# The down weights of the experts go to GpSimd's DMA queue, gate and up stay on SyncE's

## What is computed

```python
def moe_swiglu(h, w_router, wg, wu, wd):
    logits = (h @ w_router).astype(jnp.float32)
    top_v, top_i = lax.top_k(logits, TOP_K)
    ...
    act = jax.nn.silu(jnp.einsum('bnd,edf->bnef', h, wg)) * jnp.einsum('bnd,edf->bnef', h, wu)
    act = act * gates.astype(h.dtype)[..., None]
    return jnp.einsum('bnef,efd->bnd', act, wd)
```

## Time and profile before

| | us |
|---|---|
| median of 3 runs | 1752.54 |
| lowest, highest | 1752.37, 1757.84 |
| the profiled execution, its own time | 1752.99 |
| its span in the profile | 1751.2 |
| expert stage, from the first expert product to the last | about 876 to 1715 |

### The profile page before, as it was taken

The page is one execution under the profiler, slowest core; times in us unless marked ns, Lnnn a source line. Parts: engine busy times, 40 slices in busy tenths (PEclk is TensorE's granted clock), DMA queues, the critical chain, the costliest instruction groups (busy, mean ns, idle before and its releaser), DMA issues.

```text
span 1751.2 us, 24750 instructions
## 1 busy us (share of the span) xinstructions
PE 1560.6 (89%) x9147; PEld 1030.0 (59%) x9148; DVE 767.1 (44%) x1243; ACT 583.8 (33%) x994; POOL 75.9 (4%) x92
## 2 busy tenths in 40 slices
PE   4798989999999898989687999899998999999771
PEld 1684577888887585567522566545654677676220
DVE  0574676333333573766700455334453443333015
ACT  1433445233331542441200544334443333333001
POOL 2010011000000010020000000000000000000002
PEclk8899999999999899999898999999999999999885
DMA  9245536343243445465389999999999477777992
GB/s 340 97 144 169 193 110 216 119 144 117 100 144 122 144 143 188 169 207 195 108 313 389 355 388 362 388 350 360 317 371 369 173 265 262 254 270 261 395 370 80
DMA packets 202174, 414.09 MB, mean 236 GB/s; under 512 B 11336, under 2 KB 52296, under 8 KB 202032
## 3 DMA queue, kind: packets, MB, share of 16 engines
q1 hardware_dynamic: 195712, 390.64, 62.0%
q0 software_dynamic: 5264, 18.04, 3.2%
q10 hardware_dynamic: 1056, 3.54, 0.5%
HBM read 400.64 MB, written 11.53 MB: 235 GB/s over the span
## 4 chain that ended last, share of the span: by engine, by line
PE 75%; DMA 8%; DVE 6%; issue 4%; ACT 3%; SPq 2%; ACTq 1%; POOL 0%; DVEq 0%; POOLq 0%
PE ps L1966 27%; PE ps L2368 5%; PE ps L2285 5%; PE ps L2362 4%; PE ps L2286 4%; PE ps L2289 4%; DMA qkv<-in_w_moe_up 3%; PE ps L2408 3%; PE ps L2414 3%; PE ps L1898 2%; PE ps L2310 2%; DMA gu_ring<-in_w_moe_up 2%; PE ps L2313 2%; PE ps L2316 2%; SPq L679 2%
## 5 line engine op out<-in xcount | busy, mean ns | idle before, releaser
L1966 PE MATMUL ps<-d_ring_parts,scratch_parts 128*128 128x512 f32 (+1 forms) x444 | 172.4, 388 | 14.3 <-DVE hT_parts L1241 9.5
L1800 DVE TENSOR_TENSOR cst<-cst,ps 128x256 f32<-128x256 f32 (+2 forms) x89 | 32.9, 369 | 270.8 <-ACT cst L1098 270.8
L1966 PE MATMUL ps<-gu_ring_parts,scratch_parts 128*128 128x512 f32 (+1 forms) x336 | 128.0, 381 | 0.0
L1966 PE MATMUL ps<-d_ring_parts,hT_parts 128*128 128x512 f32 (+1 forms) x312 | 118.4, 380 | 0.0
L1966 PE MATMUL ps<-gu_ring_parts,o_parts 128*128 128x512 f32 x264 | 103.8, 393 | 0.0
L1966 PEld LDWEIGHTS ps<-d_ring_parts,scratch_parts 128*128 128x128 f32 x444 | 84.6, 190 | 32.5 <-issue 9.3
L2362 PE MATMUL ps<-gu_ring,hT 128*64 128x512 f32 x288 | 74.8, 665 | 30.1 <-issue 18.5
L1106 ACT ACTIVATE cst<-ps 128x128 f32<-128x128 f32 (+1 forms) x51 | 16.1, 316 | 235.4 <-PE ps L2384 221.3
L1757 DVE TENSOR_TENSOR gu_ring_parts<-gu_ring,qkv_parts 128x1024 fp32r<-128x1024 f32 x54 | 64.3, 1223 | 64.8 <-PE ps L2368 23.4
L1098 ACT ACTIVATE cst<-ps 128x256 f32<-128x256 f32 (+2 forms) x89 | 30.7, 345 | 166.3 <-PE ps L2289 74.8
L2285 PE MATMUL ps<-qkv_parts,o_parts 128*128 128x512 f32 x182 | 75.5, 415 | 4.0 <-DVE gu_ring_parts L1757 4.0
(11 more groups left out here) (414 smaller groups left out, 3369.5 us busy)
## 6 DMA issues: line engine op xcount, KB each, us to landing
gu_ring<-in_w_ada SPq DMA_DIRECT2D x48, 1024.0 KB, 7.4
gu_ring<-in_w_moe_gate SPq DMA_DIRECT2D x96, 512.0 KB, 7.9
gu_ring<-in_w_moe_up SPq DMA_DIRECT2D x96, 512.0 KB, 9.4
gu_ring<-in_w_moe_down SPq DMA_DIRECT2D x96, 512.0 KB, 9.2
d_ring<-in_w_moe_gate SPq DMA_DIRECT2D x48, 512.0 KB, 9.4
d_ring<-in_w_moe_up SPq DMA_DIRECT2D x48, 512.0 KB, 10.4
d_ring<-in_w_moe_down SPq DMA_DIRECT2D x48, 512.0 KB, 7.1
gu_ring<-in_w_in SPq DMA_DIRECT2D x16, 1024.0 KB, 7.4
```

Of the source, the lines that this page charges most:

```text
L1966: ins = pe.matmul(out, a, w, start=(start and n == 0), stop=(stop and n == 2))
```

## The change

SyncE loads gate/up granules alone, in the old order and with the old waits. GpSimd loads the down granules: 4 and 5 of the first expert after `out_mm` reaches 12, granule 10 after its load of norm parameters, and the rest in a loop of its own with registers of its own for the experts' numbers. `freed` is unchanged but for the engine that waits. Each of the 33 positions has its own landing semaphore in place of one for each of the 11 slots. The early gathers keep their place in GpSimd's stream, behind what is loaded there now. Which slot a position has, and which products run in which order, stays.

```diff
-        ring_landed = [sem(f"ring_landed{k}") for k in range(RING)]
+        ring_landed = [sem(f"granule_landed{k}") for k in range(GRANULES)]
...
+        def freed(eng, t, pos):
...
+            kind, _, _, k = granule_of(pos)
+            if kind == "gu":
+                eng.wait_ge(gu_freed, t * GU_GRANULES + (k + 1))
+            elif pos == GRANULES - 1:
+                eng.wait_ge(y_mm, t * HELD + HELD)
+            else:
+                eng.wait_ge(d_freed, t * D_GRANULES + (k + 1))
...
             sp.wait_ge(out_mm, 12)
-            for pos in range(RING):
-                if pos == 9:
-                    sp.wait_ge(gather_mm, 16)
-                load_granule((0, 0), pos)
+            for pos in GATE_UPS:
+                if pos < RING:
+                    if pos == 9:
+                        sp.wait_ge(gather_mm, 16)
+                    load_gate_up((0, 0), pos)
...
+                now = experts_of(sp, t)
+                for pos in GATE_UPS:
+                    if pos >= RING:
+                        freed(sp, t, pos - RING)
+                        load_gate_up(now, pos)
...
-                else:
-                    pool.wait_ge(gather_mm, 16)
                 if l == 0:
                     rstds(3, 1)
                 else:
+                    pool.wait_ge(out_mm, 12)
+                    for pos in (4, 5):
+                        for f in range(2):
+                            pool.dma_start(ring[pos][:, D * f:D * f + D],
+                                           w_moe_down[0, 0][FC * (pos - 4) + P * f:FC * (pos - 4) + P * f + P, :]
+                                           ).then_inc(ring_landed[pos], 16)
+                    pool.wait_ge(gather_mm, 16)
                     load_ln(1, 1)
+            DOWNS = [pos for pos in range(GRANULES) if granule_of(pos)[0] == "d"]
+
+            def load_down(experts, pos):
+
+                _, sc, q, _ = granule_of(pos)
+                e = experts[sc % 2 if sc < NSUPER - 1 else 0]
+                for f in range(2):
+                    r0 = FS * sc + FC * q + P * f
+                    pool.dma_start(ring[pos % RING][:, D * f:D * f + D], w_moe_down[0, e][r0:r0 + P, :]).then_inc(
+                        ring_landed[pos], 16)
+
+            load_down((0, 0), 10)
+            pool.wait_ge(sched_ready, 1)
+            with nc.Fori(0, NE - 1, engines=[pool.engine], hint_back_edge=True) as t:
+                now = experts_of(pool, t)
+                for pos in DOWNS:
+                    if pos >= RING:
+                        freed(pool, t, pos - RING)
+                        load_down(now, pos)
+                then = experts_of(pool, t + 1)
+                for pos in DOWNS:
+                    if pos < RING:
+                        freed(pool, t, pos + GRANULES - RING)
+                        load_down(then, pos)
...
             pool.wait_ge(rows_placed, 1)
             pool.wait_ge(rows_out, STORES * NE)
...
-                        act.wait_ge(ring_landed[pos % RING], t * (32 * (GRANULES // RING)) + 32 * (pos // RING + 1))
+                        act.wait_ge(ring_landed[pos % GRANULES], t * 32 + 32 * (pos // GRANULES + 1))
```

More of the change, by code:

```diff
@@ L669, in _, with load_gate_up @@
                             d_landed[ch % D_SLOTS], 16)
-            def load_granule(experts, pos):
-                kind, sc, q, _ = granule_of(pos)
+            def load_gate_up(experts, pos):
+                _, sc, q, _ = granule_of(pos)
                 e = experts[sc % 2 if sc < NSUPER - 1 else 0]
[L675 to L681, removed]
-                else:
-                    for f in range(2):
-                        r0 = FS * sc + FC * q + P * f
-                        sp.dma_start(dst[:, D * f:D * f + D], w_moe_down[0, e][r0:r0 + P, :]).then_inc(landed, 16)
@@ L687, in freed @@
[L687 to L699, removed]
@@ L701, in _ @@
-            sp.wait_ge(out_mm, 12)
-            for pos in range(RING):
-                if pos == 9:
-                    sp.wait_ge(gather_mm, 16)
-                load_granule((0, 0), pos)
+                dst, landed = ring[pos % RING], ring_landed[pos]
+                nk, w = (2, FS) if sc < NSUPER - 1 else (4, FC)
+                for a, src in enumerate((w_moe_gate[0, e], w_moe_up[0, e])):
+                    sp.dma_start(dst.rearrange("p (k a f) -> p k a f", k=nk, a=2)[:, :, a, :],
+                                 src.rearrange("(k p) f -> p k f", p=P)[:, nk * q:nk * q + nk, FS * sc:FS * sc + w]
+                                 ).then_inc(landed, 16)
@@ L706, in _ @@
+            GATE_UPS = [pos for pos in range(GRANULES) if granule_of(pos)[0] == "gu"]
+            sp.wait_ge(out_mm, 12)
+            for pos in GATE_UPS:
[3 more added lines that the diff above has]
+                    load_gate_up((0, 0), pos)
             sp.wait_ge(sched_ready, 1)
             with nc.Fori(0, NE - 1, engines=[sp.engine], hint_back_edge=True) as t:
[L708 to L719, removed]
+                now = experts_of(sp, t)
[3 more added lines that the diff above has]
+                        load_gate_up(now, pos)
@@ L720, in _ @@
+                then = experts_of(sp, t + 1)
+                for pos in GATE_UPS:
+                    if pos < RING:
+                        freed(sp, t, pos + GRANULES - RING)
+                        load_gate_up(then, pos)
+            now = experts_of(sp, NE - 1)
+            for pos in GATE_UPS:
+                if pos >= RING:
+                    freed(sp, NE - 1, pos - RING)
+                    load_gate_up(now, pos)
             for i in range(NT):
@@ L800, in _ @@
                 else:
-                    load_ln(1, 1)
+                    pool.wait_ge(out_mm, 12)
[5 more added lines that the diff above has]
+                    pool.wait_ge(gather_mm, 16)
+                    load_ln(1, 1)
+            DOWNS = [pos for pos in range(GRANULES) if granule_of(pos)[0] == "d"]
+            def load_down(experts, pos):
+                _, sc, q, _ = granule_of(pos)
+                e = experts[sc % 2 if sc < NSUPER - 1 else 0]
[8 more added lines that the diff above has]
+                for pos in DOWNS:
+                    if pos >= RING:
+                        freed(pool, t, pos - RING)
+                        load_down(now, pos)
+                then = experts_of(pool, t + 1)
+                for pos in DOWNS:
+                    if pos < RING:
+                        freed(pool, t, pos + GRANULES - RING)
+                        load_down(then, pos)
+            now = experts_of(pool, NE - 1)
+            for pos in DOWNS:
+                if pos >= RING:
+                    freed(pool, NE - 1, pos - RING)
+                    load_down(now, pos)
             pool.wait_ge(rows_placed, 1)
```

7 lines of the change are left out of this document (5 added, 2 removed).

## The result

| | before | after |
|---|---|---|
| median | 1755.19 us (4 runs) | 1787.57 us (4 runs, 1779.41 to 1797.07) |
| ratio | | 1.0172, 95% interval 1.0130 to 1.0214 |
| profiled execution, its span | 1752.99, 1751.2 us | 1786.47, 1784.7 us |
| second set of runs (11 and 6) | 1759.47 us | 1784.09 us, ratio 1.0148 (1.0121 to 1.0175) |

The change makes the kernel 1.5 to 1.7% slower. I had forecast 1757 us in a range of 1744 to 1770; the result lies outside. In the changed kernel L679 has become L693 and L685 L817; L2362, L2368, L2384, L2408, L2414 and L2477 each stand 36 lines further down (L2398, L2404, L2420, L2444, L2450, L2513), as do L807, L1727 and L1822 (L843, L1763, L1858).

The account below looks back on a forecast made before the run. TensorE was taken as the busiest engine (89%), with narrow experts bound by DMA bytes. Terms 0 + 0 + 0 + 0 + 4.5 us on the profiled 1752.99 us gave 1757.5, or 1757 us beside the median; range 1744 to 1770 us.

Parts of the forecast that it names:

- Issue: Expert stage: 176 down DMAs move to GpSimd at 0.58 us each, no stall; SyncE's saved issues were hidden: 0.
- semaphores: Landing of granules: 33 semaphores in place of 11, with the same number of waits: 0.
- VectorE beside: Each expert's three VectorE copies could lock out GpSimd's DMAs, by the skill's rule at most 1.7 us an expert.
- How the two queues share: Expert stage: downs issued after a gate/up can overtake it; taken as 0, ends -7 and +16 us.
- In byte-bound experts it is 0 for the same reason: Narrow experts: overtaking costs 0, since the load backlog outlasts TensorE's work to free the next slots.
- My backlog of 8 us: At an overtaken fourth gate/up granule: three granules queued, longer than the 5.7 us TensorE needs to free the next slots.
- Wide experts: loads land long before use.: Wide experts, where TensorE is always busy: overtaking by downs costs 0.
- Gathers: Last expert: early gathers behind GpSimd's last downs delay VectorE's folds and the result's copy: +4.5 us, ends 0 and +12.
- Rival 1: Expert stage: downs rob gate/ups of bandwidth; new waits at 975 to 1145 us exceed twice 6.7 us; 1773 us, chance 0.12.
- The general signs of a wrong forecast: Gate/up waits below 20 or above 45 us, any down wait, slow GpSimd DMAs, narrow experts above 400 or below 380 GB/s.
- Rival 4: Two TensorE idle times, if code loading, grow 4 us each through a third party at the engines: 1765 us, chance 0.06.
- rival 2: Expert stage: faster, with fewer gate/up waits and holes, 401 GB/s and folds at the low end: 1740 us, chance 0.17.

Follow-up runs that it names:

- sems: The kernel before with one landing semaphore for each of the 33 granules, all loads still on SyncE's queue: 1757.20 us, ratio 0.9999.
- hold_next: The changed kernel with only the next expert's downs (granules 4, 5, 10) held until its gate/up granule 3 or 9 has landed: 1774.08 us, 1.0074.
- in_turn: The changed kernel, but GpSimd issues a down only after SyncE has issued every gate/up ahead of it: 1772.40 us, ratio 1.0072.
- the repeat: The changed kernel run once more, unaltered, beside a later group of runs: 1784.09 us, ratio 1.0148.
- half_rows: The changed kernel, each down DMA carrying one half of the columns of 256 rows, runs of 2 KB instead of 4: 1800.95 us, 1.0247.
- swap: The changed kernel with queues exchanged: GpSimd loads gate/ups, SyncE downs, early gather 0 ahead of granule 30: 1810.46 us, ratio 1.0290.
- both: The kernel before, each granule's first DMA by SyncE, second by GpSimd, old order, gathers 0 and 1 ahead of granule 28: 1776.11 us, 1.0127.

## Why the prediction was wrong

- **Issue, semaphores, VectorE beside: right.** 0.59 us a down DMA against the forecast 0.58, and no pause like the 10.31 us of the earlier trace rows. sems is at 0.9999. The lock that the Trainium skill (SBUF — State Buffer, "DVE blocks DMA") warns of would hold up GpSimd's DMAs. All 172 down DMAs at L817 took 0.53 to 0.54 us each, so no trace of it shows here.
- **How the two queues share: the step that failed.** I had written 0, with ends of -7 and +16 us. The case in it was right: a gate/up overtaken by downs, 5.4 us late. Granule 21 is that case, 16.4 - 11.0 = 5.4 us. That it meets the forecast's 5.4 us so exactly is luck, since the shares were not equal. Four things in it were wrong. (1) "In byte-bound experts it is 0 for the same reason": the first expert, byte-bound, lost 11.4 us, more than any other place but one. (2) I let only the two downs of the same super overtake. But a queue that does not wait for gate/ups runs on to the next expert, and beside granule 31 there were five downs. hold_next and in_turn put this at about half of the whole loss. (3) I argued that a late TensorE costs nothing since the engines work on bytes that must be moved anyway. They do until the ring is full; then the share falls to 0.58 over 30 us where it was 0.91. A ring bounds how far ahead a queue can work, so work done early on the wrong half is lost when the right half is late. My backlog of 8 us was compared with TensorE's next few steps and not with the time until the ring is full. (4) I assumed shares of one half each. The queues took turns by packets, so in bytes it was 2.0 to 1 for GpSimd's, and 3.7 to 1 beside granules 30 and 31, where the three longest waits lie. I had the lengths of the rows and did not use them.
- **"Wide experts: loads land long before use."** No wait for weights there before; after, 8.9 us in eight waits from 1362 to 1657 us, and the third group is 13.0 us longer, the largest item: 8.9 us of these waits, 4.2 us more busy time, 2.1 us more idle time with no releaser shown at the start of the last expert, less 2.2 us of a wait for VectorE that is gone. I had no term for it.
- **The clock: missed.** No term of the sum turned longer waits into slower matmuls; busy time rose by 13.1 us (6.5 in the repeat), part of it in the clock's dip behind the longest wait.
- **Gathers: the delay right, the path not.** The first gather went behind the last downs, and VectorE's fold waited for it, as forecast. But the 4.5 us of the sum were the copy of the result, delayed by VectorE's third fold; this copy (1749.94 us) waited 2.83 us for TensorE and not for a fold. The 4.50 us that appeared are a wait of TensorE's last turn, for which I had 1.6 us (1709.75 to 1711.3), and 3.65 us of them are VectorE's idle time with no releaser shown. That both are 4.5 is luck. The last expert as a whole is 2.2 us longer.
- **Rival 1** (gate/up robbed, 1773 us) was the true case in its mechanism, to which I gave 0.12, but not in its place, and its bound of 16 us was too small. Its own test failed: TensorE's gate/up waits from 975 to 1145 us are 3.4 us, not above twice 6.7; the loss is at the ends of experts and in the third group. The general signs of a wrong forecast, waits for gate/ups above 45 us and any wait for a down, came true: 47.9 and 4.9.
- **Rival 4** (code loading, two longer idle times) did not come true: the idle times before the first products of the first and the last expert are 9.97 and 10.52 us, 20.5 in total, against 18.5 before and 20.1 in sems, which has one queue.
- **Rule on issuing engines.** I used the rule of the Trainium skill (DMA: Bandwidth & Descriptors, Issuing engines are not separate DMA queues) that more issuing engines only save issue time against rival 2. That they gain no rate holds here (394 to 396 GB/s after, 393 before, in narrow experts). It does not say that they cost nothing; what the page says on taking queues in turn, which I had not weighed, bears on that.

Still open: the rest of in_turn's 0.7% (the two queues should still share by packets in it, but no run takes that away alone), what GpSimd's queue costs as such, and why half_rows and swap are so slow. No kernel of the study beat the one before.

## What to carry to other kernels

A stream of loads in order of use on one queue is a schedule, and a second queue removes it: whatever is not waited for runs ahead as far as the ring lets it, and in a byte-bound stage that is taken from the one load that the compute engine stands on. If two queues are wanted, tie their issue order together with a count (here that gave half of the loss back); if one is enough, keep it. If they are loaded at the same time, work out their shares from the sizes of their packets in a trace: the queue with the smaller packets gets the smaller share. When costing an overtaking, ask how far the free queue can run, not only what stands next to the late load, and add the slower clock behind each long wait.

## What the runs showed of the hardware

- Where two queues had work, they moved equal numbers of packets: 351 and 352, 426 and 427 in the changed kernel, 271 and 273 in swap. In bytes that was 2.0 to 1, 3.7 to 1 and 1 to 1, by the sizes of the packets. In both, equal loads in the same order landed with medians of 9.1 us (GpSimd's) and 12.5 us (SyncE's).
- GpSimd's packets stayed at 3.6 KB whether its runs were 4 KB or 2 KB; SyncE's were 1.75 KB on average over the changed kernel, whose gate/up runs are 2 KB, and 1 KB in granules 30 and 31.
- One DMA of SyncE's held its queue for 7.79 us (at 914.10, behind a row of others); GpSimd's 172 down DMAs took 0.53 to 0.54 us each all through the stage, so a backlog on SyncE's side did not slow GpSimd's issue.
